# One block of a depthwise convolution goes from TensorE to GpSimd, tap by tap

## The reference

```
def conformer_conv(xn, pw1_w, pw1_b, dw_w, dw_b, ln_g, ln_b, pw2_w, pw2_b):
    a, g = jnp.split(xn @ pw1_w + pw1_b, 2, axis=-1)
    h = a * jax.nn.sigmoid(g)
    h = depthwise_conv(h, dw_w) + dw_b
    h = jax.nn.silu(layernorm(h, ln_g, ln_b))
    return h @ pw2_w + pw2_b
```

## Time and profile before

| | us |
|---|---|
| median of 3 runs (2162.83 to 2163.39) | 2163.27 |
| the profiled execution | 2164.69 |
| its span in the trace | 2162.7 |
| PE busy | 2125.1 (98%) |
| VectorE busy | 1701.4 (79%) |
| ScalarE busy | 1356.1 (63%) |
| GpSimd busy | 98.2 (5%) |

### The profile page before, as it was taken

How to read it: one execution, slowest core, us unless ns; L and a number is a source line. 1 busy time by engine, 2 the same in 40 slices (tenths; PEclk the granted TensorE clock), 3 DMA queues, 4 the chain that set the end, 5 groups by cost and what they waited for, 6 DMA issues and landing times. The chain is left out here.

```text
span 2162.7 us, 30608 instructions
## 1 busy us (share of the span) xinstructions
PE 2125.1 (98%) x11850; PEld 1827.8 (85%) x11850; DVE 1701.4 (79%) x1512; ACT 1356.1 (63%) x1161; POOL 98.2 (5%) x113
## 2 busy tenths in 40 slices
PE   8999999999999999999999999999999999999998
PEld 8998999888888888888888888888889988788886
DVE  5655555697588888888888888888877674888887
ACT  5454433545477777777777777777757344577775
POOL 1010000020000000000000000000000000000000
PEclk9999999999999999999999999999999999999999
DMA  9462555674389999999999999999954252799995
GB/s 320 172 180 98 176 188 177 225 213 163 133 300 394 370 394 375 381 380 373 382 368 389 365 390 359 394 373 382 383 203 166 78 205 78 266 378 388 376 379 223
DMA packets 281528, 623.91 MB, mean 288 GB/s; under 512 B 11128, under 2 KB 42048, under 8 KB 281184
## 3 DMA queue, kind: packets, MB, share of 16 engines
q1 hardware_dynamic: 270800, 586.76, 74.2%
q0 software_dynamic: 10640, 35.91, 5.5%
HBM read 604.98 MB, written 14.16 MB: 286 GB/s over the span
## 5 line engine op out<-in xcount | busy, mean ns | idle before, releaser
L2632 DVE TENSOR_TENSOR w_low<-ring,w_high 128x2048 fp32r<-128x2048 f32 x426 | 971.4, 2290 | 130.0 <-ACT w_high L1824 129.0
L1824 ACT ACTIVATE w_high<-ring 128x2048 fp32r<-128x2048 f32 x426 | 815.3, 1917 | 166.8 <-PE ps L884 166.8
L883 PE MATMUL ps<-w_high,parts 128*128 128x512 f32 x1928 | 747.5, 388 | 0.0
L882 PE MATMUL ps<-w_high,parts 128*128 128x512 f32 x1560 | 616.9, 395 | 1.5 <-DVE parts L2312 1.4
L884 PE MATMUL ps<-w_low,parts 128*128 128x512 f32 x1560 | 608.5, 390 | 0.0
L883 PEld LDWEIGHTS ps<-w_high,parts 128*128 128x128 f32 x1928 | 362.6, 188 | 70.2
L2016 DVE TENSOR_TENSOR w_low<-ring,w_high 128x2048 fp32r<-128x2048 f32 (+2 forms) x123 | 275.7, 2255 | 94.3 <-ACT w_high L1538 93.2
L882 PEld LDWEIGHTS ps<-w_high,parts 128*128 128x128 f32 x1560 | 293.1, 188 | 63.9 <-issue 5.9
L884 PEld LDWEIGHTS ps<-w_low,parts 128*128 128x128 f32 x1560 | 292.8, 188 | 62.6
L1538 ACT ACTIVATE w_high<-ring 128x2048 fp32r<-128x2048 f32 (+2 forms) x123 | 231.2, 1884 | 139.6 <-PE ps L884 129.8
L882 PE MATMUL ps<-XT_high,w_high 128*128 128x256 f32 x1056 | 301.8, 286 | 5.3 <-DVE parts L2007 3.5
(11 more groups left out here) (463 smaller groups left out, 1505.7 us busy)
## 6 DMA issues: line engine op xcount, KB each, us to landing
ring<-in_od_moe_gu SPq DMA_DIRECT2D x224, 1024.0 KB, 8.2
ring<-in_od_moe_down SPq DMA_DIRECT2D x112, 1024.0 KB, 8.2
ring<-in_w SPq DMA_DIRECT2D x96, 1024.0 KB, 8.6
ring<-in_ev_ffn_gu SPq DMA_DIRECT2D x22, 1024.0 KB, 7.2
ring<-in_xa_wkv SPq DMA_DIRECT2D x8, 2048.0 KB, 8.5
ring<-in_od_pw_w SPq DMA_DIRECT2D x6, 2048.0 KB, 9.7
ring<-in_w_in SPq DMA_DIRECT2D x6, 2048.0 KB, 8.4
ring<-in_ev_ffn_down SPq DMA_DIRECT2D x11, 1024.0 KB, 5.0
```

The costliest lines, as they stand in the source:

```text
L882: mm(out_, xh, wh, start=start, stop=False)
L883: mm(out_, xl, wh, start=False, stop=False)
L1824: A(w_high[:, (j + split_from[k]) % SPLITS, :], ring[:, j % NS, :], ACT.Copy).then_inc(moe_sem(k, "high"), 1)
L2632: V.tensor_tensor(w_low[:, place, :], ring[:, j % NS, :], w_high[:, place, :].bitcast(F32), SUB)\
```

## The change

Block 2 leaves TensorE. GpSimd makes it with 61 instructions: one for the first tap with the bias, then for each of 30 taps a multiplication into a scratch tile (`TAPPED`, which is `RST`, free at that time) and an addition to `CO`. Each waits for the one before it on the new semaphore `pool_taps`. They stand in GpSimd's queue ahead of the copies of blocks 6 and 7 and begin when `glu` is at 1. TensorE makes five blocks, 3 to 7; VectorE builds five sets of diagonals; SP issues the 16 copies of block 3 alone. VectorE waits for `pool_taps` before it adds block 2 to the channel sum. Two older semaphores become one, `small_operands_ready`.

```
@@ -38,6 +38,8 @@
 GROUPS_OF_32 = 4
 STEPS = 8
 DVE_BLOCKS = 2
+POOL_BLOCK = 2
+BY_TAP = 3
 SHIFTED = 256 + SHIFTS * (STEPS - 1)
 PADDED = 288
 MASKED = -1e30
@@ -105,7 +107,7 @@
 VEC_TILES = -(-sum(r for _, r in VECTORS) // P)
 VEC_ROWS = sum(r for _, r in VECTORS)
 TAPS_AT = VEC_TILES * P
-TAP_COLS = (8 - DVE_BLOCKS) * STEPS * GROUPS_OF_32 + DVE_BLOCKS * CONV
+TAP_COLS = (8 - BY_TAP) * STEPS * GROUPS_OF_32 + BY_TAP * CONV
 VEC_LOADS = sum((VEC_AT[n] + r - 1) // P - VEC_AT[n] // P + 1 for n, r in VECTORS)
 
 
@@ -114,8 +116,8 @@
 
     taps = np.zeros((SHIFTS * STEPS, D), np.float32)
     taps[:CONV] = np.asarray(w).reshape(CONV, D)
-    on_pe = taps.reshape(STEPS, SHIFTS, KC, GROUPS_OF_32, 32)[:, :, DVE_BLOCKS:].transpose(1, 4, 2, 0, 3).reshape(P, -1)
-    on_dve = taps[:CONV].reshape(CONV, KC, P)[:, :DVE_BLOCKS].transpose(2, 1, 0).reshape(P, -1)
+    on_pe = taps.reshape(STEPS, SHIFTS, KC, GROUPS_OF_32, 32)[:, :, BY_TAP:].transpose(1, 4, 2, 0, 3).reshape(P, -1)
+    on_dve = taps[:CONV].reshape(CONV, KC, P)[:, :BY_TAP].transpose(2, 1, 0).reshape(P, -1)
     return np.ascontiguousarray(np.concatenate([on_pe, on_dve], 1))
 
 
@@ -559,12 +561,12 @@
             for i in range(n_dense):
                 if i == unit_panel[UNIT["Bv0"]]:
                     sync.wait_ge(S("xs_ready"), 3)
-                    shift_copies(sync, (2, 3))
+                    shift_copies(sync, (3,))
                 if i == unit_panel[UNIT["pw2_0"]]:
                     sync.wait_ge(S("glu"), 2)
                     shift_copies(sync, (4, 5))
                 if i == unit_panel[UNIT["Bo0"]]:
-                    sync.wait_ge(S("features_made"), 7)
+                    sync.wait_ge(S("features_made"), 6)
                     sync.dma_start(KEY_WEIGHTS, k_major(ins["mem_wk_2"], 0, 0, T)).then_inc(S("lone_half_landed"), 16)
                 load(i, i >= SLOTS)
             gu1, dn1 = ins["od_moe_gu"], ins["od_moe_down"]
@@ -676,6 +678,17 @@
                 pool.dma_start(dst, src.partition_broadcast(P)).then_inc(S("small_loaded"), 16)
             row(0, ins["od_pw2_b"][0].partition_broadcast(P))
             memory(5, "mem")
+            pool.wait_ge(S("glu"), 1)
+            b, G, TAPPED = POOL_BLOCK, nc.gpsimd, RST
+            step = Steps(pool, S("pool_taps"))
+            for k in range(CONV):
+                at = TAPS_AT + TAP_COLS - (BY_TAP - b) * CONV + k
+                wv = cols[:, at:at + 1]
+                if k == 0:
+                    step(G.tensor_scalar(CO[:, b, :], HC[:, b, 0:T], wv, vec("od_dw_b", b), ALU.mult, ALU.add))
+                else:
+                    step(G.tensor_scalar(TAPPED, HC[:, b, k:k + T], wv, None, ALU.mult))
+                    step(G.tensor_tensor(CO[:, b, :], CO[:, b, :], TAPPED, ALU.add))
             pool.wait_ge(S("glu"), 2)
             shift_copies(pool, (6, 7))
             row(0, ins["od_norm_moe"][0].partition_broadcast(P))
@@ -1079,10 +1092,10 @@
             project("value1")
             memory_projections("B", "xs_ready", 3)
 
-            for n in range(KC - DVE_BLOCKS):
-                b = n + DVE_BLOCKS
+            for n in range(KC - BY_TAP):
+                b = n + BY_TAP
                 pe.wait_ge(S("taps_built"), n + 1)
-                pe.wait_ge(S(f"shifted{b // 2}"), 16 * 2 * SHIFTS * GROUPS_OF_32)
+                pe.wait_ge(S(f"shifted{b // 2}"), 16 * (1 if b == 3 else 2) * SHIFTS * GROUPS_OF_32)
                 if n >= 3:
                     pe.wait_ge(S("features_by_act"), n - 2)
                 for i in range(STEPS):
...
@@ -2348,7 +2361,7 @@
 
                 for k in range(first, end):
                     for kc in range(DVE_BLOCKS):
-                        at = TAPS_AT + TAP_COLS - (DVE_BLOCKS - kc) * CONV + k
+                        at = TAPS_AT + TAP_COLS - (BY_TAP - kc) * CONV + k
                         wv = cols[:, at:at + 1]
                         if k == 0:
                             last = V.tensor_scalar(CO[:, kc, :], HC[:, kc, 0:T], wv, vec("od_dw_b", kc), MUL, ADD)
@@ -2403,15 +2416,18 @@
             build_taps(0)
             build_taps(1)
             lows(halves_to("Bv0"))
-            for n in range(2, KC - DVE_BLOCKS):
+            for n in range(2, KC - BY_TAP):
                 taps(3 * n + 10, 3 * n + 13)
                 build_taps(n)
-            taps(28, CONV)
+            taps(3 * (KC - BY_TAP) + 10, CONV)
             step(V.tensor_tensor(CHANNEL_SUM, CO[:, 0, :], CO[:, 1, :], ADD))
             for b in range(2, KC):
                 if b == KC - 1:
                     lows(halves_to("Bv1", -1))
-                dve.wait_ge(S("features_by_act"), b - 1)
+                if b == POOL_BLOCK:
+                    dve.wait_ge(S("pool_taps"), 2 * CONV - 1)
+                else:
+                    dve.wait_ge(S("features_by_act"), b - 2)
                 add = V.tensor_tensor(CHANNEL_SUM, CHANNEL_SUM, CO[:, b, :], ADD)
                 if b < KC - 1:
                     step(add)
@@ -2422,7 +2438,7 @@
                 part = CO[:, 4 * i:4 * i + 4, :]
                 V.scalar_tensor_tensor(part, rep(ps[:, 7, 0:T], 4), -1.0 / D, part, MUL, ADD).then_inc(S("features_by_vector"), 1)
             dve.wait_ge(S("features_by_vector"), 3)
-            dve.wait_ge(S("features_by_act"), KC)
+            dve.wait_ge(S("features_by_act"), KC - BY_TAP + 2)
             step(V.tensor_tensor(SQ[:, 0:4, :], SQ[:, 0:4, :], SQ[:, 4:8, :], ADD))
             V.tensor_tensor(SQ[:, 0:2, :], SQ[:, 0:2, :], SQ[:, 2:4, :], ADD).then_inc(S("sums_built"), 1)
             dve.wait_ge(S("sums_ready"), 3)
...
```

More of the change, by code:

```diff
@@ L1115, in route @@
                     turn_by_tokens(src, ready, value)
-                pe.wait_ge(S("router_split"), 1)
+                pe.wait_ge(S("small_operands_ready"), 1)
                 E, G = MOES[k]["experts"], MOES[k]["groups"]
@@ L1278, in fox_sums @@
             def fox_sums():
-                pe.wait_ge(S("fox_log"), 1)
+                pe.wait_ge(S("small_operands_ready"), 2)
                 mm(ps[:, 7, 496:500], upto, logf_fox[:, 0, :], start=True, stop=True)
@@ L2294, in _ @@
                 last = V.tensor_tensor(both[:, :, e:2 * e], raw, both[:, :, 0:e].bitcast(F32), SUB)
-            last.then_inc(S("router_split"), 1)
+            last.then_inc(S("small_operands_ready"), 1)
             def ffn_gate(f):
@@ L2728, in _ @@
             step(V.tensor_tensor(logf_fox, logf_fox, ffa, SUB))
-            V.tensor_scalar(minus_logf, logf_fox, -1.0, None, MUL).then_inc(S("fox_log"), 1)
+            V.tensor_scalar(minus_logf, logf_fox, -1.0, None, MUL).then_inc(S("small_operands_ready"), 1)
             cs = ffa
```

## The result

The changed kernel takes 2200.78 us (median of 5 runs, 2200.38 to 2201.88), the one before 2163.27: a ratio of 1.0174, 95% interval 1.0163 to 1.0185. That is +37.5 us, where +22.4 was forecast; 2200.78 lies above the range of 2160 to 2200. The profiled execution took 2200.76 us with a span of 2198.4. One execution of them all, the profiled one of the first experiment's kernel, took 9342 us; no run shows why, that ratio leaves it out, and that kernel's rows come from a second run.

A forecast was written before the change was run, and what follows sets the result against it. TensorE was taken as the bound in the convolution, VectorE close behind. GpSimd's taps ending at 484.3 make the convolution end 19.05 us later; with 3.4 for the clock, +22.4 gives 2186 us, range 2160 to 2200.

The forecast's parts named there:

- The price of one instruction: One of GpSimd's 61 tap instructions: 0.50 us plus 0.04 for the semaphore, 0.54 us alone.
- the forecast's own range: Whole kernel: 2179 to 2195 us, from 0.42 to 0.62 us a turn instead of 0.50.
- The turns: GpSimd and VectorE taps: one at a time, 40 pairs alternate, pushing VectorE back 0.50 us each, 20 us.
- T: End of GpSimd's taps for block 2, forecast at 484.3 us on the timeline.
- sign of turns: VectorE's taps up to 484: near a microsecond each if the engines take turns, 0.48 us if not.
- The copies' chain: Behind GpSimd's taps: last copy issued 15.65 us later, landing 3.0 us after that, then TensorE's two blocks, 6.9 us.
- T + 25.55: End of TensorE's convolution if it waits for the copies of blocks 6 and 7; forecast at 509.85.
- 3.4 for the clock: TensorE after standing 22.7 us: the granted clock falls, which adds 3.4 us once.
- The largest gain, 3.0 us: TensorE's lost block, 3.45 us, less a 0.5 us wait for the channel sum, if all added work is hidden.
- the first rival: GpSimd calculates beside VectorE and quickly: T = 456.6, gain 3.0 us, time 2160.3; chance 0.18.
- VectorE's push-back: VectorE's taps: delayed 20 us by turns, ending at 508.0, hidden inside TensorE's wait for the copies.
- beside and slow: GpSimd slower than 0.62 us an instruction, VectorE's rows unchanged, only copies late: 2174 at 0.8 us; chance 0.18.

The follow-up runs named there:

- the first experiment's kernel: Changed kernel with SyncE instead of GpSimd issuing the copies of blocks 6 and 7: 2181.97 us, ratio 1.0086; executed again for its rows: 2182.95 us.
- the half of the taps: Changed kernel, but GpSimd makes 15 of block 2's 31 taps and 16 are left out: 2166.58 us, ratio 1.0017.
- The best form: Changed kernel, block 7's copies on SyncE, block 6's on ScalarE, and GpSimd's product a two-input multiplication with the tap broadcast: 2178.79 us, ratio 1.0074.

## Why the prediction was wrong

*The price of one instruction is the step that failed.* "I take 0.50 us [...] and 0.04 for the semaphore: 0.54 alone." Measured alone: 0.92 from start to start on average, the product 0.92 and 1.01 from start to start, the addition 0.74 and 0.83. 61 of them are 55.8 us and not 32.9: 22.9 us too few. The row that I took it from, the spacing of plain issues, is not arithmetic; the one row of arithmetic on this shape, VectorE's addition of 0.43 us, was used as the lower end. With both ends open, 0.45 to 2.23 us, the forecast's own range should not have stopped at 0.62.

The Trainium skill (GPSIMD Engine Reference, Elementwise — side-by-side cycle accounting) gave 0.55 us for an addition by the estimate in the prediction; the measured 0.74 is a third longer, and the measurement decides.

*The turns were nearly right in sum and wrong in kind.* I had 40 pairs that alternate one to one, T = 484.3 of which 27.7 us are waiting (60.6 − 32.9). Measured: 22.0 us (77.8 − 55.8), 19.2 of them behind VectorE's splits and diagonals, 2.8 beside the rest. The forecast's sign of turns was a VectorE tap near a microsecond; it became 0.66. Short ones overlap: GpSimd's two pairs from 480.29 to 484.08, 3.6 us alone, and VectorE's six taps from 479.53 to 483.50, 2.9 alone, take 4.6 us together and not 6.5.

The Trainium skill (SBUF — State Buffer, Who interferes with whom) says that a VectorE instruction with two SBUF inputs contends with a GpSimd instruction that reads SBUF, not with one that only writes. GpSimd's memsets bear out the second half (taps of 0.481 us), and the slower taps (0.655) agree with the first. But VectorE's long memsets, which have no input, cost GpSimd 7.5 us as well, and that whole instructions exclude each other holds here for the long ones only.

*T and the copies.* T is 17.2 us late, 501.5 against 484.3: +22.9 by the price, −5.7 by the turns. The copies' chain is as forecast: the last of the 32 is issued 16.0 us after the last tap (15.65 and 0.3 in front of the first), and TensorE starts 1.3 us after that (517.53 to 518.85), below my 3.0. That the wait is the copies is shown by moving them (2181.97, 2178.76) and by the half of the taps (no wait at T = 463.1).

*The sum, from T on.* 501.5 + 0.3 + 15.7 + 1.3 + 9.7 = 528.5, and 528.57 was measured. The forecast's T + 25.55 and 3.4 for the clock make 530.4 from the measured T; landing was 1.7 too long, the clock 0.6. So T's 17.2 us less these 1.9 make the whole miss of 15.1 (37.5 − 22.4), within 0.2.

*The largest gain, 3.0 us, was wrong too.* I had looked at the loads behind block 2's copies, and not at the copies of blocks 4 and 5, which are wanted 3.45 us earlier and don't come earlier. It had no part in the forecast, but in the first rival: with quick and harmless GpSimd work the time is 2163.8, not 2160.3.

*VectorE's push-back* was 20 us and is 15: its taps end at 503.08 (495.94 + 7.14; 508.0 forecast). It lies inside the wait for the copies, as the prediction said, and comes out as soon as they are moved: the 15.5 us that remain at 2178.8 are about as much.

Of the rivals *beside and slow* comes nearest in price, 0.92 us an instruction; by its own arithmetic it would have ended at T = 479.8, and the waits behind the splits came on top. Neither way alone gave the range: price and turns were rivals in the text, and they add.

## What to carry to other kernels

Before an engine gets its first arithmetic in a kernel, nothing in the trace prices it; a range must then run to both ends, and rivals that can hold at the same time (a high price, and turns) must also be added up. What stands behind new work in an in-order queue is part of its price: here 32 transfers made a late result of one block into a wait of 30 us for two others. Taking a block from the bound engine is worth no more than what the next operand allows, so read for each following step when its data come.

## What was not expected of the hardware

- On GpSimd, 128x256 in float32, a `tensor_scalar` with one operation takes 0.92 us and the same with two 0.56. The addition of two tiles takes 0.74, the two-input multiplication with the tap broadcast over the columns 0.61, a memset 0.31. The best form's product, where nothing holds it up:

```profile
432.42 0.61 POOL L690 TENSOR_TENSOR work<-work,cols 128x256 f32<-128x256 f32 x1
```

- A GpSimd instruction that reads can wait out two VectorE splits in a row (4.96 us at 440.35), while VectorE's taps lose 0.17 us each to a GpSimd that loses hardly anything to them.
- TensorE's clock fell behind a pause of 2.57 us: the granted clock was 1.00 from 500 to 518 with transposes and 0.63 and 0.81 in the windows that follow.
